# Merged parameter and tail transposes, gate and value chunks in turn, dt between the halves, and other PSUM banks in the router of a hybrid decoder step

## The reference

```
proj = rmsnorm(x, ln_mix) @ w_in          # columns: u_a | u_b | z | x,B,C | dt
u    = u_a * sigmoid(u_b)
v, conf_tail = causal_dwconv(conf_buf, u, 31 taps)     # tail: last 30 rows of u are an output
v    = silu(layernorm(v))
xbc, ssm_tail = causal_dwconv(ssm_buf, xbc, 4 taps)    # tail: last 3 rows of xbc are an output
xbc  = silu(xbc)
dt   = softplus(dt_raw + dt_bias)
y    = ssd_scan(xs, dt, -exp(a_log), B, C) + d_skip * xs
y    = grouped_rmsnorm(y * silu(z)) * ssm_norm_g
x    = x + concat(v, y) @ w_out
h    = rmsnorm(x, ln_ffn)
logits of 4 groups and of 32 experts; top-1 group, top-2 experts in it
x    = x + sum over the chosen experts of weight * ((silu(h@w_gate) * (h@w_up)) @ w_down)
return rmsnorm(x, ln_final), and the new convolution rows and scan states
```

## Time and profile before

| | |
|---|---|
| median of 3 runs | 797.75 us (797.67 to 797.92) |
| the profiled execution's own time | 798.58 us |
| its span, first to last instruction | 796.9 us |
| PE busy | 763.7 us (96%) |
| DVE, ACT, POOL busy | 272.6, 156.8, 139.7 us |
| moved by DMA | 249.58 MB, mean 313 GB/s |
| granted PE clock over the span | 0.987 of full speed |

### The profile page before, as it was taken

How to read it: one execution, slowest core, us unless ns; L and a number is a source line. 1 busy time by engine, 2 the same in 40 slices (tenths; PEclk the granted TensorE clock), 3 DMA queues, 4 the chain that set the end, 5 groups by cost and what they waited for, 6 DMA issues and landing times.

```text
span 796.9 us, 8780 instructions
## 1 busy us (share of the span) xinstructions
PE 763.7 (96%) x3510; PEld 365.7 (46%) x3510; DVE 272.6 (34%) x626; ACT 156.8 (20%) x312; POOL 139.7 (18%) x168
## 2 busy tenths in 40 slices
PE   5999999999999999899999999999999999899896
PEld 4777677767853335544333333333333333233332
DVE  2059999996646522521011101100110111010003
ACT  3310121225632002200121011111111210110122
POOL 2079899712002000100000000000000000000000
PEclk9999999999999999789999999999999999999999
DMA  9894200040839686899999999999999999999992
GB/s 271 305 378 168 106 21 0 1 114 5 288 133 296 212 302 287 300 379 403 427 426 425 428 427 426 426 428 424 428 425 429 427 425 429 426 424 430 425 381 71
DMA packets 51400, 249.58 MB, mean 313 GB/s; under 512 B 6982, under 2 KB 24422, under 8 KB 38671
## 3 DMA queue, kind: packets, MB, share of 16 engines
q1 hardware_dynamic: 45604, 243.41, 76.4%
q10 hardware_dynamic: 3227, 2.80, 1.3%
q0 software_dynamic: 2528, 2.79, 1.2%
HBM read 246.87 MB, written 8.61 MB: 321 GB/s over the span
## 4 chain that ended last, share of the span: by engine, by line
PE 93%; DVE 2%; DMA 2%; issue 2%; ACT 1%; SPq 0%; DVEq 0%; POOLq 0%
PE bank L1221 28%; PE bank L807 20%; PE bank L1244 14%; PE bank L1085 9%; PE bank L1269 9%; PE bank L1204 2%; DMA ring<-in_w_in 1%; PE bank L1233 1%; PE bank L1074 1%; PE bank L1043 1%; PE bank L909 1%; PE bank L1222 1%; DVE region_a L1648 1%; PE bank L1056 0%; PE bank L920 0%
## 5 line engine op out<-in xcount | busy, mean ns | idle before, releaser
L807 PE MATMUL bank<-region_a,ring 128*128 128x320 f32 x576 | 159.7, 438 | 2.1 <-DMA ring<-in_w_in 2.1
L1648 DVE TENSOR_TENSOR region_a<-region_a,bank 64x512 f32<-64x512 f32 (+1 forms) x33 | 22.4, 680 | 376.9 <-ACT region_a L1575 376.9
L1222 PE MATMUL bank<-ring,zz 128*64 128x512 f32 x320 | 142.0, 598 | 0.0
L807 PEld LDWEIGHTS bank<-region_a,ring 128*128 128x128 f32 x576 | 110.1, 193 | 48.6 <-issue 5.1
L1221 PE MATMUL bank<-ring,zz 128*64 128x512 f32 x288 | 127.3, 595 | 1.0 <-issue 1.0
L1649 DVE SCALAR_TENSOR_TENSOR bank<-region_a,par,bank 128x256 f32<-128x256 f32 x232 | 91.2, 480 | 0.0
L760 POOL DMA_INDIRECT region_a<-hn_scratch,region_a x16 | 15.9, 996 | 373.2 <-PE bank L1204 358.4
L1269 PE MATMUL bank<-zz,masks 128*128 128x512 f32 (+1 forms) x192 | 77.2, 603 | 0.7 <-ACT zz L1581 0.7
L1221 PEld LDWEIGHTS bank<-ring,zz 128*64 128x64 f32 x288 | 38.1, 137 | 80.7 <-issue 80.0
L1085 PE MATMUL bank<-ring,x_v_y 128*128 128x512 f32 (+1 forms) x192 | 74.0, 605 | 0.0
L1575 ACT ACTIVATE region_a<-bank 64x512 f32<-64x512 f32 x32 | 18.9, 590 | 270.1 <-PE bank L1222 270.1
(11 more groups left out here) (320 smaller groups left out, 785.8 us busy)
## 6 DMA issues: line engine op xcount, KB each, us to landing
ring<-in_expert_w_up SPq DMA_DIRECT2D x20, 2048.0 KB, 24.6
ring<-in_expert_w_gate SPq DMA_DIRECT2D x17, 2048.0 KB, 29.9
ring<-in_expert_w_down SPq DMA_DIRECT2D x16, 2048.0 KB, 34.7
ring<-in_w_in SPq DMA_DIRECT2D x9, 2048.0 KB, 20.1
x_v_y<-in_expert_w_down SPq DMA_DIRECT2D x6, 2048.0 KB, 33.2
x_v_y<-in_expert_w_gate SPq DMA_DIRECT2D x5, 2048.0 KB, 34.2
ring<-in_w_out SPq DMA_DIRECT2D x4, 2048.0 KB, 7.8
xcx<-in_expert_w_gate SPq DMA_DIRECT2D x4, 2048.0 KB, 31.2
```

The costliest lines, as they stand in the source:

```text
L807: ins = pe.matmul(pt[0:m, 0:T], w[:, k, :], ht[:, k, :], start=k == 0, stop=k == KD - 1)
L1222: ins = pe.matmul(to[CAP:P, :], x[:, k, :], wu[:, FE * k:FE * k + FE], **st)
L1648: tt_ = lambda out, a, b, op: dve.tensor_tensor(out, a, b, op)
```

## The change

Nine edits, all of order, merging or placement:

- **Parameters.** The small convolution's rows, its state rows and the long convolution's rows are loaded one under another into one tile of 64 rows, so that 8 transposes of 64 rows and 4 of 29 rows replace 8 of 35, 12 of 5 and 12 of 24 rows.
- **Tails.** The last 30 prompt rows of `u` and the 64 sample rows lie side by side, so that 8 transposes do what 16 did; for x, B, C the last 3 prompt rows likewise, 12 instead of 24.
- **Gate and value in turn.** `ub` and `ua` alternate in pairs of chunks. The parameter transposes stand behind the first two pairs. DVE waits for the copy of the long convolution's taps alone (semaphore `par`).
- **dt** is projected between the halves, its transposes stand behind the last `ua` chunk.
- **Loads.** `ln_mix` is issued by ACT; the parameters are issued behind the second weight load; ACT's small loads wait for the first weights (`ring_in[0]`), `wdt` follows them ahead of ACT's first table load, and `keep_out` goes behind the last `ua` chunk.
- **POOL** does its taps in three batches (4, 8, 6) between gates instead of 1, 1, 1, 8, 1, 1, 1.
- **Silu ahead of z.** Each silu of four x, B, C chunks stands ahead of the eviction of a z chunk instead of behind it.
- **Banks.** The router's last five jobs have fixed banks; the round robin before them shifts, since there are fewer jobs.
- **Router.** `logits` waits for each half of the transposed rows by itself, the gain of the sample rows is applied ahead of the reciprocal, and `first_max` has 3 fused instructions where it had 2 wider ones.

```
@@ bank_jobs
-        own = range(4 * half, 4 * half + 4)
-        jobs += [(("in", "b", c), "act") for c in own]
+        for c0 in (4 * half, 4 * half + 2):
+            jobs += [(("in", b, c), "act") for b in "ba" for c in (c0, c0 + 1)]
+            if c0 == 0:
+                jobs += [(("par",), "act"), (("spar",), "act")]
+                jobs += [(("cst", h, q), "act") for h in range(2) for q in range(2)]
         if half == 0:
-            jobs += [(("par",), "act"), (("spar",), "act")]
-            jobs += [(("cst", h, q), "act") for h in range(2) for q in range(2)]
-        jobs += [(("in", "a", c), "act") for c in own]
-    jobs += [(("in", "dt", 0), "act")]
+            jobs += [(("in", "dt", 0), "act")]
+        else:
+            jobs += [(("dtT",), "act")]
@@ bank_table
-    fixed = {("yos",): 2, ("mean",): 3}
+    fixed = {("yos",): 2, ("mean",): 3, ("h2", 2, 0): 1, ("h2", 2, 1): 2, ("lg2",): 0, ("rank",): 1,
+             ("first",): 0, ("slots",): 2}
@@ sync: loads
-            sp_.dma_start(lnmix[:, :], A["ln_mix"].rearrange("a (p k) -> (a p) k", k=KD)).then_inc(S("mix_in"), 16)
...
-                if n == 0:
+                if n == 1:
                     ld = lambda dst, src: sp_.dma_start(dst, src).then_inc(S("par_in"), 16)
@@ gpsimd
-                for _ in range(8 if c == 3 else 1 if c < NC - 1 else 0):
+                for _ in range({1: 4, 3: 8, 5: 6}.get(c, 0)):
@@ tensor: parameters_T
+                n = N_SPAR + N_PAR
                 for c in range(NC):
-                    ins = pe.transpose(pt[:, N_PAR * c:N_PAR * (c + 1)], pst[:, P * c:P * c + P],
-                                       ident[0:N_PAR, 0:N_PAR])
+                    ins = pe.transpose(pt[:, n * c:n * c + n], vf[0:n, P * c:P * c + P], ident[0:n, 0:n])
                 ins.then_inc(filled, 1)
                 pt = take(pe, "spar")
-                for c in range(XC_N):
-                    pe.transpose(pt[:, 5 * c:5 * c + 5], sst[:, P * c:P * c + P], ident[0:5, 0:5])
-                    ins = pe.transpose(pt[:, 60 + 24 * c:84 + 24 * c], sstate[:, P * c:P * c + P], ident[0:24, 0:24])
+                n = N_SPAR
+                for c in range(XC_N - NC):
+                    ins = pe.transpose(pt[:, n * c:n * c + n], vf[0:n, P * (NC + c):P * (NC + c) + P], ident[0:n, 0:n])
@@ tensor: projections
-                for c in range(4 * half, 4 * half + 4):
-                    project(("in", "b", c), f"ub{half}", c % 4)
+                for c0 in (4 * half, 4 * half + 2):
+                    for b in "ba":
+                        for c in (c0, c0 + 1):
+                            project(("in", b, c), f"u{b}{half}", c % 4)
+                    if c0 == 0:
+                        parameters_T()
...
-                    for q in range(2):
-                        pt = take(pe, "ut", q)
...
-                pt = take(pe, "xtail", q)
...
@@ tensor: logits
-                after_read(pe, "h2", r, 1)
                 for k in range(KD):
+                    if k % 4 == 0:
+                        after_read(pe, "h2", r, k // 4)
@@ scalar
+            act.dma_start(lnmix[:, :], A["ln_mix"].rearrange("a (p k) -> (a p) k", k=KD)).then_inc(S("mix_in"), 16)
...
+            act.wait_ge(ring_in[0], 16)
             ld = lambda dst, src: act.dma_start(dst, src).then_inc(S("ssm_in"), 16)
...
+            act.wait_ge(filled, J[("xt", 2, 1)] + 1)
+            act.dma_start(wdt, w_in[:, :, C_DT:C_DT + H]).then_inc(S("wdt_in"), 16)
+            glu_parts(0)
...
+            glu_parts(4)
+            glu_parts(6)
+            act.dma_start(O["new_conf_conv_sample"][0, :, 0:HIST - TB, :], A["state_conf_conv"][0, :, TB:HIST, :])\
+                .then_inc(S("keep_out"), 16)
+            pt = got(act, "dtT")
...
-            for q in range(3):
-                z_tile(3 + q, ACT.Silu)
+
+            def x_silu(q):
                 act.wait_ge(S("xconv"), 4 * q + 4)
                 v = xc[:, 4 * q:4 * q + 4, 0:TP]
                 act.activation(v, v, ACT.Silu).then_inc(S("xact"), 1)
+
+            x_silu(0)
+            z_tile(3, ACT.Silu)
+            x_silu(1)
+            z_tile(4, ACT.Silu)
+            x_silu(2)
+            z_tile(5, ACT.Silu)
@@ vector: router
             biased("lg", range(2))
+            h2_gain(2)
             inverse(2)
-            h2_gain(2)
...
-                link(tt_(tmp_, vals, wide(mx, w), ALU.is_equal))
-                link(tt_(tmp_, tmp_, bc(desc.unsqueeze(1), [P, 3, w]), ALU.mult))
+                for r in range(3):
+                    ins = stt(tmp_[:, r, :], vals[:, r, :], col(mx)[:, r:r + 1], desc, ALU.is_equal, ALU.mult)
+                link(ins)
```

More of the change, by code:

```diff
@@ L1373, in _ @@
             ld(lnffn[:, :], A["ln_ffn"].rearrange("a (p k) -> (a p) k", k=KD))
-            act.dma_start(O["new_conf_conv_sample"][0, :, 0:HIST - TB, :], A["state_conf_conv"][0, :, TB:HIST, :])\
-                .then_inc(S("keep_out"), 16)
-            for c in range(4):
-                pt = got(act, "in", "b", c)
-                act.activation(sig[c], pt[:, 0:T], ACT.Sigmoid).then_inc(free["act"], 1)
-            pt = got(act, "par")
-            act.activation(par[:, :, :].rearrange("p c r -> p (c r)"), pt[:, 0:NC * N_PAR], ACT.Copy)\
-                .then_inc(free["act"], 1)
@@ L1384, in _, with glu_parts @@
-            pt = got(act, "spar")
-            act.activation(spar[:, :, :].rearrange("p c r -> p (c r)"), pt[:, 0:60], ACT.Copy)
-            act.wait_ge(S("consts"), 1)
-            for c in range(XC_N):
-                ins = act.activation(xb_seq[:, c, :, 0:SH],
-                                     pt[:, 60 + 24 * c:84 + 24 * c].rearrange("p (b t) -> p b t", b=NB), ACT.Copy)
-            ins.then_inc(free["act"], 1)
+            def glu_parts(c0):
+                for c in (c0, c0 + 1):
+                    pt = got(act, "in", "b", c)
+                    wait(act, S("glu"), c - 3)
+                    act.activation(sig[c % 4], pt[:, 0:T], ACT.Sigmoid).then_inc(free["act"], 1)
+                for c in (c0, c0 + 1):
+                    pt = got(act, "in", "a", c)
+                    wait(act, S("glu"), c - 1)
+                    act.activation(uac[c % 2], pt[:, 0:T], ACT.Copy).then_inc(free["act"], 1)
@@ L1424, in _ @@
                 act.activation(xb[:, c, SH:SH + TP], pt[:, 0:TP], ACT.Copy)
-                act.activation(xs[:, c, :], pt[:, TP:T], ACT.Copy).then_inc(free["act"], 1)
-                if c == 0:
-                    pt = got(act, "dtT")
-                    for r in range(3):
-                        ins = act.activation(dtk[:, r, :], pt[:, H * r:H * r + H], ACT.Copy)
-                    ins.then_inc(free["act"], 1)
+                act.activation(xs[:, c, :], pt[:, TP - SH:T], ACT.Copy).then_inc(free["act"], 1)
                 if c == 3:
@@ L1463, in _ @@
             z_tile(1, ACT.Silu)
-            for q in range(3):
-                rows_out(xtail_rows, got(act, "xtail", q), q)
             act.wait_ge(S("conv_s"), 1)
```

108 lines of the change are left out of this document (49 added, 59 removed).

## The result

The kernel before and after ran 20 times each on one chip. Before: median 797.83 us (796.21 to 800.97). After: median 792.76 us (791.19 to 797.58 without one disturbed run). The ratio is 0.9942, 95% interval 0.9929 to 0.9954: 0.6% or some 4.6 us faster (the two medians differ by 5.1). The profiled execution after took 791.2 us (span 789.4), 7.4 less than the one before (798.58). A profile is one execution; the runs of after scatter up to 797.6, and that the profiled pair differs by more than the medians is the first thing to explain.

A forecast was written before the change was run, and what follows sets the result against it. The weight stream sets the end and moves with PE's time up to the first expert; 0.3 + 1.2 + 2.2 + 2.5 - 0.7 + 1.2 = 6.7 us off, forecast 791.0 us, range 789.0 to 794.0.

The forecast's parts named there:

- Start: PE's first projection: with `ln_mix`'s issue gone from ahead of them, the first weights land 0 to 0.6 us earlier; -0.3.
- Parameter transposes: PE from L815 to the next projection: fewer, merged transposes take 2.70 to 2.99 us against 4.00; -1.2.
- Tails: PE's 8 transposes of L857 (0.87) and 12 of L976 (1.31) go; -2.2 us.
- Silu ahead of z: PE's waits before the second half of `scan_x` and before `scan_a`, 1.04 and 1.47 us, both go; -2.5.
- Mean's bank: z chunk 3 and the mean share bank 3, so PE waits for ACT's eviction of z; +0.7 us (0.6 to 1.7).
- Router: Bank wait of 0.60 us ends, logits begin 0.6 earlier; DVE's `biased` heads the chain to the gather; -1.2 (-0.6 to -1.4).
- ACT was not held: Rival at the start: `wdt`'s issue behind five small loads holds ACT's evictions; released later than 39, slower than before; chance 0.06.
- The waits at the scan: Rival: `keep_out`'s issue keeps 3.28 us or DVE is held otherwise, PE's waits stay; gain 4.2, 793.6; chance 0.13.
- The stream followed: Rival denied here: weight loads limited from before 335 us, the stream doesn't follow; gain 2 to 4, 794.8; chance 0.07.
- The clock: Rival: first expert's matmuls fall into a half-speed stretch, 1 to 2 us go; 792.5; chance 0.12.
- the first paragraph: Opening on the bound: in the expert loop PE falls behind its loads by 2.2 us a pair and runs dry near the end.

The follow-up runs named there:

- the repeat: The changed kernel run once more, unchanged, beside the kernel before: median 794.53 us, ratio 0.9960.
- the run that ends it: Changed kernel with z chunk 3 in bank 5 and the mean alone in bank 3: 792.82 us, ratio 0.9941 to the kernel before.

## Why the prediction was right, and where not

Forecast 791.0, range 789.0 to 794.0; median 792.76.

- **Start, -0.3.** First projection at 12.54 for 13.49, 0.95 earlier, more than forecast. The profile then gained 2.5 us more, for the projections ran at full speed from the first (17.46 us for 19.92; up to 17 us the profile before has 3 of their matmuls in a microsecond, the one after 5 or 6). But that is a matter of the execution: in the repeat they took 19.16, with a granted clock of 0.50 from 14 to 17 us, and on the kernel before with the new router 19.04. It also bought nothing, for at their end PE waits for the parameters. I said of these loads "wanted at 33" and gave no landing; they land at 31.8 to 33.6. This is the missing row of my sum: it caps the start, and it makes it scatter. The next projection starts at 34.7 to 35.7 in eight of the ten profiles with this start, at 37.7 and 38.1 in the two whose parameters came last (there the transposes of 120 rows also took 3.12 and 3.46 us for 1.86), and at 37.4 and 36.4 with the old start: mostly 1 to 2 us, where the forecast had 1.5.
- **Parameter transposes, 2.7 to 3.0 us:** 2.86.
- **Tails, -2.2:** 0.87 and 1.31 gone, as written.
- **Silu ahead of z, -2.5:** shown by its own run, 2.50. I made it depend on DVE's lead and on `keep_out`'s issue (1.29 us, I took 0.5); the run with the silus behind z shows that DVE's lead alone gives nothing. The order without the lead was not run, but by the rows it would not have been enough: the last chunks ended at 179.0 before, and PE now wants their silu at 174.83. DVE was earlier than forecast: dt at 92.87 for 93.7, the last chunks at 170.0 for 173.9.
- **Mean's bank, +0.7:** 0.62, shown by the run that ends it.
- **Router, -1.2: the step that failed.** Up to the biased logits PE and DVE gained as forecast: from ACT's squaring of the sample rows (320.95, now 313.79) to `biased` it is 2.70 us for 4.56, of which 0.81 are the clock in the logits, so 1.05 for the 1.2 of the sum. What failed is that this "heads the chain to the gather" undiminished: the first expert comes no earlier than with the old router (table above), and in the times the edits measured +2.8 us on the kernel before (1.5 to 4.0) for -1.2; undone in the changed kernel, the median fell by 0.9 to 2.7. One thing that I overlooked is in this text: "The reciprocal comes 0.4 us later, hidden: the normed rows it feeds are stored long before the gather needs them." I checked the reciprocal and not what else the earlier logits release: a 2 MB load, which overtook the store. The margin from landing to gather was 335.25 - 327.9 = 7.3 us and became 327.02 - 325.2 = 1.8. But with that load put behind the store again the time did not come back (792.75 and 792.85 us), so what makes the edits cost time stays open.
- **Rivals.** ACT was not held: `wdt`'s issue took 0.59 us, ACT was free at 16.24 for the 26 that I reckoned. The waits at the scan did not stay. The stream followed. The clock: 0.50 and 0.52 in the windows from 325 to 335, but the first expert came earlier than forecast all the same (332.95 for 334.4), and its first matmul took 1.09 us for 1.08, so it was no slower there than before.

One reading of the first paragraph is the wrong way round, without weight for the sum: with 29.5 us for the weights of a pair and 27.3 for PE it is the loads that fall behind PE, not PE behind its loads.

That the time came out near is in part luck: two errors of opposite sign, start and router, met in the sum. In the medians the forecast was 1.8 us too low, which is within what the router's failed step measured; that it is its cause is argued, not shown.

## What to carry to other kernels

When an edit makes an instruction earlier, list every DMA that its semaphore releases, and ask what small transfer it now overtakes: look at the margin from that transfer's landing to its reader, not at the engine's idle time. Where two edits could both have removed a wait (an order on one engine, a lead on another), undo each: here the lead without the order gave nothing, and the order without the lead was left untried. Where a part is made of several edits, time them apart: the router's four were not, and its loss has no cause. And where one profile shows a gain larger than the medians, compare the same stretch in several executions before believing its parts.

## What was not expected of the hardware

- The placing of the ten parameter loads (1.3 MB in all) ahead of one 2 MB load delayed that load's landing to 34.6 us (without them PE uses it from about 21 us with no wait), and between 24 and 28 us, with loads outstanding, the DMA engines were busy only 0.23 at 58 GB/s. I can't explain the idle share.

```profile
24.00:28.00 4.00, 1.58 (x6) 0.76 (x4) 0.00 (x0) 0.44 (x1) 0.00 (x0) 1.00 0.23 58
```

- A 256 KB store took 4.0 to 4.9 us (6.7 once) with a 2 MB load issued 1.2 to 1.7 us behind it, and 7.2 to 10.3 us with the load between 0.4 us ahead of it and 0.3 behind, on another engine's queue.
- The clock: after PE's wait of 3.13 us for the parameters in the run with the small loads late, the 16 transposes of 120 rows took 3.46 us for 1.86 at full clock, the granted clock being 0.54 from 32 to 36 us, so most of that window was at the level of 1.2 GHz. From the first parameter transpose to the next projection it was 4.84 us for 2.69 after the change, where PE had waited 1.96 us: 2.2 us lost beside the wait itself. The window:

```profile
32.00:36.00 4.00, 2.71 (x18) 2.54 (x19) 1.13 (x3) 1.57 (x16) 0.07 (x1) 0.54 0.89 310
```
